# A second set of seven block products in the feed-forward pairs of a two-block transformer kernel

## The reference, cut to what matters

```python
hf = rms_norm(x, g_ffn)
x = x + (jax.nn.silu(hf @ w_gate) * (hf @ w_up)) @ w_down
```

## Time and profile before

| | |
|---|---|
| median of 3 runs | 2374.46 us (2371.44 to 2374.56) |
| profiled execution, own time | 2376.75 us |
| its span, first to last instruction | 2375.0 us |
| PE, DVE, ACT, POOL busy | 2365.2, 1861.1, 1193.0, 188.4 us |
| granted TensorE clock | 1.0 |
| unit copies to w_hi / subtractions to w_lo | 795 / 796 |

### The profile page before, as it was taken

One profiled execution on the slowest core, in us unless ns is written; L12 is line 12 of the kernel. 1 busy time (PEld: TensorE's weight loads), 2 busy tenths in 40 slices (PEclk: granted clock), 3 DMA queues, 4 the chain that ended last, 5 costly groups with the idle time before them and its releaser, 6 DMA issues.

```text
span 2375.0 us, 30803 instructions
## 1 busy us (share of the span) xinstructions
PE 2365.2 (100%) x10764; PEld 1968.8 (83%) x10764; DVE 1861.1 (78%) x2518; ACT 1193.0 (50%) x1615; POOL 188.4 (8%) x146
## 2 busy tenths in 40 slices
PE   9999999999999999999999999999999999999999
PEld 7988888788888888888888888888888888888887
DVE  7788887877677866878897977987867786687885
ACT  6554555544444544545564445454444454454563
POOL 1000000100211212100000000010121111210000
PEclk9999999999999999999999999999999999999999
DMA  8655555565655555656556564566565565564655
GB/s 304 238 173 186 168 169 174 189 212 188 202 195 197 195 187 195 206 167 199 184 194 195 181 221 160 194 223 195 187 204 195 195 195 189 193 211 161 208 192 168
DMA packets 126495, 462.24 MB, mean 195 GB/s; under 512 B 13712, under 2 KB 14352, under 8 KB 125728
## 3 DMA queue, kind: packets, MB, share of 16 engines
q1 hardware_dynamic: 116736, 421.32, 53.7%
q0 software_dynamic: 9344, 38.85, 4.8%
q10 hardware_dynamic: 288, 0.33, 0.0%
HBM read 458.35 MB, written 2.10 MB: 194 GB/s over the span
## 4 chain that ended last, share of the span: by engine, by line
PE 97%; DVE 2%; ACT 0%; DMA 0%; issue 0%; SPq 0%; ACTq 0%; DVEq 0%
PE acc L602 66%; PE pt L602 11%; PE po L602 11%; PE acc L750 2%; PE pt L750 2%; PE po L750 1%; PE acc L951 1%; PE acc L607 1%; PE po L934 1%; PE acc L865 1%; PE po L926 1%; DVE w_lo L1614 0%; PE pt L905 0%; PE acc L880 0%; DVE tmp_b L1749 0%; DVE tmp_c L1749 0%
## 5 line engine op out<-in xcount | busy, mean ns | idle before, releaser
L1614 DVE TENSOR_TENSOR w_lo<-raw,w_hi 128x1024 fp32r<-128x1024 f32 x796 | 992.2, 1258 | 424.8 <-ACT w_hi L1106 417.9
L1106 ACT ACTIVATE w_hi<-raw 128x1024 fp32r<-128x1024 f32 x795 | 836.6, 1058 | 936.1 <-PE acc L602 605.6
L602 PE MATMUL acc<-w_hi,norm_hi 128*128 128x512 f32 (+1 forms) x1524 | 593.6, 390 | 0.3 <-ACT w_hi L1106 0.2
L602 PE MATMUL acc<-w_hi,norm_lo 128*128 128x512 f32 (+1 forms) x1524 | 590.2, 388 | 0.0
L602 PE MATMUL acc<-w_lo,norm_hi 128*128 128x512 f32 (+1 forms) x1524 | 404.9, 388 | 0.9 <-DVE w_lo L1614 0.9
L602 PEld LDWEIGHTS acc<-w_hi,norm_hi 128*128 128x128 f32 x1524 | 286.1, 188 | 59.2 <-ACT w_hi L1106 1.0
L602 PEld LDWEIGHTS acc<-w_lo,norm_hi 128*128 128x128 f32 x1524 | 284.8, 188 | 60.3 <-DVE w_lo L1614 2.2
L602 PEld LDWEIGHTS acc<-w_hi,norm_lo 128*128 128x128 f32 x1524 | 286.2, 188 | 57.6
L602 PE MATMUL acc<-w_hi,mix_hi 128*128 128x512 f32 x848 | 330.9, 390 | 1.3 <-DVE mix_lo L2100 1.1
L602 PE MATMUL acc<-w_hi,mix_lo 128*128 128x512 f32 x848 | 330.0, 389 | 0.0
L602 PE MATMUL acc<-w_lo,mix_hi 128*128 128x512 f32 x848 | 226.8, 389 | 0.0
(11 more groups left out here) (312 smaller groups left out, 2513.7 us busy)
## 6 DMA issues: line engine op xcount, KB each, us to landing
raw<-stream SPq DMA_DIRECT2D x795, 512.0 KB, 3.5
heads<-seven_in POOLq DMA_DIRECT2D x24, 1024.0 KB, 6.7
heads<-x_in POOLq DMA_DIRECT2D x4, 512.0 KB, 8.3
x<-x_tok POOLq DMA_DIRECT2D x4, 512.0 KB, 7.3
x<-mem_tok POOLq DMA_DIRECT2D x2, 1024.0 KB, 6.6
x<-x_tok POOLq DMA_DIRECT2D x1, 2048.0 KB, 8.7
heads<-rows_in POOLq DMA_DIRECT2D x2, 1024.0 KB, 9.4
heads<-decay_in POOLq DMA_DIRECT2D x4, 512.0 KB, 5.3
```

The costliest lines, as they stand in the source:

```text
L602: last = pe.matmul(out_[:, c * NB:c * NB + width], a[:, k * T + c * P:k * T + (c + 1) * P], w[:, s, kk * width:(kk + 1) * width], start=cl ...
L1106: act.activation(w_hi[:, (units.fixed - 1) % RING, :], src, ACT.Copy).then_inc(w_hi_ready, 1)
L1614: dve.tensor_tensor(w_lo[:, s, :], src, w_hi[:, s, :].bitcast(F32), ALU.subtract)\
```

## The change

In the 24 pairs, the second unit of each block is also done by seven products. `STEPS = 2` sets now lie side by side in `heads`. Per pair PE has: `open_seven` with 8 products (24 matmuls, two steps of 12, the second behind a wait of its own), `close_seven` with 2 products (one for each set, 6 matmuls) and, in the same function, two units from the stream, each holding two tiles and used by 2 products (6 matmuls). Then 12 ordinary units of 12 matmuls. The pair still has 14 units in the stream. POOL loads 8 tiles (2 MB, in three DMAs) once `open_seven` of the pair before is done (`products_done`); the fourth tile of both sets lies alternately in `heads` and `tab`. DVE makes the four tile differences of the first set, between two of its splits, and POOL those of the second. ACT makes high parts in three instructions (4, 4 and 2 tiles), DVE low parts in three. The activation sums are twice as wide. Two loads (`tables`, rows of `g_final`, later `p_in` and the bias rows) and `gained_tables` move behind the last pair of their feed-forward.

Of the hunks below, those from `seven_hi` to the first `steps` lines are ACT's; those from `seven_sums` on are DVE's.

```diff
-SEVEN_CUTS = ((0, 5), (5, 7))
+SEVEN_CUTS = ((0, 4), (4, 6))
...
             def load_seven(j):
-                pool.dma_start(heads[:, L_TILE * T:L_TILE * T + 8 * NB].rearrange("p (a n) -> p a n", a=2)[:, :, 0:2 * NB],
-                               seven_in[j].rearrange("p (a n) -> p a n", a=2)).then_inc(seven_landed, 16)
+                for step in range(STEPS):
+                    pool.dma_start(raw7(step, W11, 3), seven_in[j][:, step * 4 * NB:(step * 4 + 3) * NB])\
+                        .then_inc(seven_landed[step], 16)
+                pool.dma_start(last_raw(j), seven_in[j].rearrange("p (s n) -> p s n", s=STEPS)[:, :, 3 * NB:])\
+                    .then_inc(last_landed, 16)
...
             for j in range(N_SEVEN):
                 if j:
-                    pool.wait_ge(seven_used, j)
+                    pool.wait_ge(products_done, j)
...
             def open_seven(j, act, ready):
 
                 c11, c12, c21, c22 = quarters_of(j)
                 pe.wait_ge(block_taken, first_of(j) - 2)
-                pe.wait_ge(seven_ready, 2 * j + 1)
                 pe.wait_ge(act_ready, sums_needed(j))
-                products(j, ((c11, "a11", W11), (c22, "s1", T1), (c12, "s2", T2), (c21, "s3", T3)), act, ready, True)\
-                    .then_inc(products_done, 1)
+                pe.wait_ge(*ready)
+                for step in range(STEPS):
+                    pe.wait_ge(seven_ready, 3 * j + step + 1)
+                    w = [(hi7(step, i), lo7(step, i)) for i in range(4)]
+                    last = products(j, step, ((c11, "a11", w[W11]), (c22, "s1", w[T1]), (c12, "s2", w[T2]),
+                                              (c21, "s3", w[T3])), act, step == 0)
+                last.then_inc(products_done, 1)
...
             def close_seven(j, act, ready):
 
                 c11, c12, c21, c22 = quarters_of(j)
-                pe.wait_ge(seven_ready, 2 * j + 2)
+                pe.wait_ge(seven_ready, 3 * j + 3)
                 pe.wait_ge(combined, j + 1)
                 pe.wait_ge(third_copied, j + 1)
-                products(j, ((c11, "a21", W21), (c12, "s4", W22), (c21, "a22", T4)), act, ready, False)\
-                    .then_inc(seven_used, 1)
+                pe.wait_ge(*ready)
+                for step in range(STEPS):
+                    last = products(j, step, ((c21, "a22", (last_hi()[:, step], last_lo(j)[:, step])),), act, False)
+                last.then_inc(seven_used, 1)
+                for step in range(STEPS):
+                    units.add()
+                    slot = (units.fixed - 1) % RING
+                    pe.wait_ge(w_hi_ready, units.value())
+                    pe.wait_ge(raw_read, units.value())
+                    one, two = ((w_hi[:, slot, at], w_lo[:, slot, at]) for at in (slice(0, NB), slice(NB, 2 * NB)))
+                    products(j, step, ((c11, "a12", one), (c12, "s4", two)), act, False).then_inc(w_used, 1)
...
-                            one_block(NU - 1, norm, k0=UK, token_major=True, opened=True)
-                            one_block(NU - 1, norm, k0=UK, token_major=True, opened=True,
-                                      mid=opening(pair, 3))
+                            one_block(NU - STEPS, norm, k0=STEPS * UK, token_major=True, opened=True)
+                            one_block(NU - STEPS, norm, k0=STEPS * UK, token_major=True, opened=True,
+                                      mid=opening(pair, 2))
...
             def seven_hi(j, part):
...
-                if part == 0:
-                    act.wait_ge(seven_summed, j + 1)
-                act.activation(hi7(first, n), raw7(first, n), ACT.Copy).then_inc(seven_hi_ready, 1)
+                if part < STEPS:
+                    act.wait_ge(seven_summed[part], j + 1)
+                    act.activation(hi7(part, W11, 4), raw7(part, W11, 4), ACT.Copy).then_inc(seven_hi_ready, 1)
+                else:
+                    if j:
+                        act.wait_ge(seven_used, j)
+                    act.activation(last_hi(), last_raw(j), ACT.Copy).then_inc(seven_hi_ready, 1)
...
-                            sums = {5: [lambda: sums_hi(which, False)], NU - 1: [gated]}
-                            steps(2 * NU, both(early, sums, preparing(after, 6), joining(after, 13)))
+                            sums = {7: [lambda: sums_hi(False), gated]}
+                            steps(2 * NU, both(early, preparing(after, 5, 6, 8), sums, joining(after, 13)))
...
-                            steps(2 * NU - 2, both(early, preparing(after_, 5), {NU - 2: [gated]}, sums, ready_))
+                            steps(2 * NU - 2, both(early, preparing(after_, 4, 6, 7), {NU - 1: [gated]}, sums, ready_))
...
+            def seven_sums(j):
+
+                dve.wait_ge(seven_landed[0], 16 * (j + 1))
+                dve.tensor_tensor(raw7(0, T3), raw7(0, T2), raw7(0, T1), ALU.subtract)
+                link(dve.tensor_tensor(raw7(0, T1), raw7(0, T1), raw7(0, W11), ALU.subtract))
+                link(dve.tensor_tensor(raw7(0, T2), raw7(0, T2), raw7(0, T1), ALU.subtract))
+                dve.wait_ge(last_landed, 16 * (j + 1))
+                dve.tensor_tensor(last_raw(j)[:, 0], last_raw(j)[:, 0], raw7(0, T2), ALU.subtract)\
+                    .then_inc(seven_summed[0], 1)
...
-                def preparing(j, at, behind=3):
+                def preparing(j, *at):
 
                     if j is None:
                         return {}
-                    return {at + behind: [lambda: seven_lo(j, 0)],
-                            at + behind + 1: [lambda: seven_lo(j, 1)]}
+                    return {at[0] - 2: [lambda: seven_sums(j)], **{k: [lambda i=i: seven_lo(j, i)] for i, k in enumerate(at)}}
...
-                            sums = {3: [lambda: sums_raw(which, False, which * N_SEVEN)],
-                                    6: [lambda: sums_lo(which, False)], NU - 1: [gated], 2 * NU - 1: [take_up]}
-                            steps(2 * NU, both(early, preparing(after, 5), joining(after, 13), sums))
+                            sums = {7: [lambda: sums_raw(False, which * N_SEVEN), gated],
+                                    9: [lambda: sums_lo(False)], 2 * NU - 1: [take_up]}
+                            steps(2 * NU, both(early, preparing(after, 6, 8, 10), joining(after, 13), sums))
...
-                            steps(2 * NU - 2, both(early, preparing(after, 3), sums, ready_, ends_))
+                            steps(2 * NU - 2, both(early, preparing(after, 5, 7, 8), sums, ready_, ends_))
```

More of the change, by code:

```diff
@@ L299, in two_blocks @@
         act_done = sem("act_done")
-        seven_landed = sem("seven_landed")
-        seven_summed = sem("seven_summed")
+        seven_landed = [sem(f"seven_landed{i}") for i in range(STEPS)]
+        last_landed = sem("last_landed")
+        seven_summed = [sem(f"seven_summed{i}") for i in range(STEPS)]
         seven_hi_ready = sem("seven_hi_ready")
@@ L735, in two_in_parts, with products @@
                         one_block(n_units, act, token_major=True, need=need, part=range(at, end), back=back * (i > 0))
[L737 to L741, removed]
+            def products(j, step, terms, act, clear):
+                sums = sums_at(hidden_sums(j))
+                for bank, of, (w_hi_, w_lo_) in terms:
                     if of[0] == "a":
-                        k, t = int(of[1]) - 1, int(of[2]) - 1
+                        k, t = step * UK + int(of[2]) - 1, int(of[1]) - 1
                         at = slice(k * T + t * P, k * T + (t + 1) * P)
@@ L746, in products @@
                     else:
[L747 to L750, removed]
+                        at = step * NB + (int(of[1]) - 1) * P
+                        a_hi, a_lo = (heads_r[:, (sums + i) * T + at:(sums + i) * T + at + P] for i in (0, 4))
+                    for i, (w, a) in enumerate(((w_hi_, a_hi), (w_hi_, a_lo), (w_lo_, a_hi))):
+                        last = pe.matmul(bank, a, w, start=clear and i == 0, stop=i == 2, skip_group_check=True)
                 return last
@@ L819, in mlp @@
                         else:
-                            after = lambda ki: down(ki + 1)
+                            after = lambda ki: down(ki + STEPS)
                             close_seven(j, mix, hidden_ready[g])
-                            for i, (at, end) in enumerate(SEVEN_CUTS if p == 0 else ((0, nd - 1),)):
+                            for i, (at, end) in enumerate(SEVEN_CUTS if p == 0 else ((0, nd - STEPS),)):
                                 for back in (1, 0):
-                                    one_block(nd - 1, mix, k0=UK, token_major=True, need=after, part=range(at, end),
-                                              back=back * (i > 0), opened=True,
-                                              mid=opening(pair, 4 if p == 0 else 2) if not i + back else None)
+                                    then = None
+                                    if (i, back) == ((1, 1) if p == 0 else (0, 0)):
```

(14 more changed lines are left out.)

148 lines of the change are left out of this document (87 added, 61 removed).

## The result

| | median us | runs | profiled execution, span |
|---|---|---|---|
| before | 2374.41 | 4 | 2376.75, 2375.0 |
| after | 2395.64 (2392.72 to 2397.22) | 4 | 2395.52, 2393.7 |

The change makes the kernel slower: 1.0091 of the time before, interval 1.0078 to 1.0103, or +21.2 us. 2396.8 was forecast.

The account below looks back on a forecast made before the run. PE bounds the kernel: number of matmuls times their distance, plus its waits. -16.3 - 1.8 + 27.6 + 1.6 + 11.2 = +22.3 us makes the median 2396.8; range 2372 to 2411, the forecast's own 2387 to 2411.

Parts of the forecast that it names:

- waits in g0 down 1 gone: Two waits at the openings in g0 down 1, for late tiles, vanish because POOL loads earlier: -1.8 us.
- 12 transposing pairs: Six pairs per feed-forward that also transpose wait 2.3 us each, 27.6; g1 up 3 starts late, 1.6 more.
- g0 up 1, twice: Once per feed-forward, PE waits 2.6 at unit 12 and 3.0 at the opening; 5.6 taken, twice: 11.2 us.
- first pair: First 2 MB load of each feed-forward, against gained_tables leaving it: taken as nothing, between -1 and +3.
- The order as the cause: DVE's work fits the fullest pair as a sum; program order behind the transposes makes PE wait.
- Both waits per pair: Transposing pairs: 0.4 to 1.2 us for w_hi of unit 9, another 1.27 for w_lo of unit 10.
- The forecast's formula: Unit 9's w_hi comes at X + 6.9, wanted at 20.40; unit 10's w_lo adds 1.27: 1.7 to 3.0 us.
- X: End of the transposes in a transposing pair, counted from the close's first matmul: between 13.9 and 15.2 us.
- Rival C: POOL's doubled load displaces the stream, X moves by 1 to 2 in 12 pairs: 2415 us; chance 0.05.
- It fits as a sum; the order decides: DVE's load in the fullest pair reaches 41.9 of 42.2 us, so instruction order decides.
- Rival A: The sums are never waited for, only the matmuls count: 2374.5 - 18.1 = 2356.4 us; chance 0.11.
- Rule of the port: VectorE two-input and GpSimd SBUF instructions exclude each other; one meeting costs 0.87 us, a second up to 0.5 more.

Follow-up runs that it names:

- order_only: Changed kernel; in the up pairs ACT's first-set high parts moved behind split 5, DVE's low parts behind splits 6, 7, 8: 2371.76 us, 0.9992 of the kernel before.
- sums_early: Changed kernel, g0 up 1 alone reordered: activation sums ahead of the transposes, tile parts mostly one split later; 2382.61 us, 1.0037 of the kernel before.
- with both: Changed kernel with the reorderings of order_only and sums_early, and DVE's tile sums behind split 4: 2360.61 us, 0.9945 of the kernel before.
- dve_both: Changed kernel with DVE making the tile sums of both sets, one behind the other, and POOL none: 2403.55 us, 1.0126 of the kernel before.
- load_late: Changed kernel with POOL issuing its loads behind the close (seven_used), not behind products_done: 2448.63 us, 1.0325 of the kernel before.
- pool_both: Changed kernel with POOL making the tile sums of both sets and DVE none, positions unchanged: 2376.77 us, 1.0011 of the kernel before.

## Why the prediction was right

The terms, against what the pairs measured (a pair's length is the distance between the first matmuls of successive closes):

| term | predicted | measured |
|---|---|---|
| 72 matmuls | -16.3 | -16.3 (light pairs 42.84 to 42.16) |
| waits in g0 down 1 gone | -1.8 | -1.5 (32.84 and 32.53 to 31.26 and 31.24) |
| 12 transposing pairs | 27.6 + 1.6 | 26.7 (1.6 to 3.6 each) |
| g0 up 1, twice | 11.2 | 13.2 (5.8 and 7.4) |
| first pair | 0 | -3.1 in the profiles |
| sum | +22.3 | +19.0, spans +18.7 |

- The order as the cause was right: the same work in another order gives back 23.9 of the 26.7 us (order_only), 13.0 of the 13.2 (sums_early) and 35.0 with both.
- Both waits per pair were right in place and size: 0.76 and 1.28 us in g1 up 2, against 0.4 to 1.2 and 1.27. The forecast's formula, X + 6.9 - 20.4 + 1.27 (X is the end of the transposes, counted from the close), gives the extra length of every transposing pair over 42.16 to within 0.2 us, each time 0.1 to 0.2 too high: 2.0 for X = 14.20 in g1 up 2 (1.8 measured), 2.8 for 15.02 in g2 up 2 (2.6), 3.8 for 16.01 in g1 up 3 (3.6).
- X itself spread more than foreseen. It lies at 14.0 to 15.2 in ten pairs (13.9 to 15.2 forecast) and at 15.6 and 16.0 in g1 up 3. POOL began its sums 1.6 us ahead of the close to 5.5 behind it, in seven of the twelve pairs at 4 to 5.5 (4 to 6 forecast). So seven pairs have 1.6 to 1.9 us and five 2.5 to 3.6, where the forecast had 2.3 for all, and 3.1 in g1 up 3.
- Not foreseen: in those five pairs a wait of 0.6 to 1.2 us at the `w_lo` of unit 8. It is due 19.5 behind the close, and split 4, behind the sums, ends at X + 5.05, so the wait comes when X passes 14.4. It is within what the formula gives for that X, since it moves the later deadlines too. g1 up 3 has another of 0.2 and 0.6 at unit 7.
- Rival C was too small for the time, but its sign is there: copies of ACT wait for the stream's DMA, in g1 up 3 for 2.48 and 2.09 us. Beside POOL's 2 MB two stream loads took 8.5 and 8.4 us there, against 3.5 at the median. In dve_both, without sums on POOL, X is still 15.1 and 14.6 in g1 up 3 and 13.87 in the other ten, so the late stream is worth about 1 us in these two pairs; VectorE, late with the units before, has a share in it that no run separates. The copy in the first feed-forward:

```profile
769.53 1.06 ACT L1139 ACTIVATE w_hi<-raw 128x1024 fp32r<-128x1024 f32 x1 [2.48 <-DMA raw<-stream]
```

- g0 up 1 was sized at 2.6 and 3.0. In the second feed-forward it is 2.8 and 3.2. In the first the second wait is just 1.7, since unit 12 itself took 1.4 longer, on the slow clock. The slow matmuls, 1.4 and 1.6 us in the two feed-forwards, are the part of this term that the sum left out. That the sum came so close is in part luck: the transposing pairs were 2.5 us too high and g0 up 1 2.0 too low.
- "It fits as a sum; the order decides" holds. The sum itself, 41.9 us in the fullest pair, was too high: 39.0 and, in the second feed-forward, 40.0 us were measured there, in pairs of 43.95 and 44.89.
- Taking the change in the median from the profile's own waits was off by the 3 us of the first pair: the profiled execution of before was slower than most. It did no harm, since the forecast put that term at nothing and counted from the median: without the row of the first pair the measured terms give +22.1, and the medians moved by 21.2.
- Rival A had the right size for another kernel: with both orders mended the time is 2360.6, against its 2356.4.
- Rule of the port (the Trainium skill, SBUF — State Buffer, "Who interferes with whom": a VectorE instruction with two SBUF inputs and a GpSimd one that reads SBUF exclude each other): the trace agrees, but one meeting a pair at 0.87 us was not what came. Five transposing pairs have one slowed subtraction of DVE ahead of X, at 1.48 to 1.55 us instead of 1.23, and seven have two, at 1.34 to 2.31. In load_late seven of the eight sums meet.

## What to carry to other kernels

When the bound engine's work shrinks, every deadline behind it moves forward: set the helpers' order against the new timetable, unit by unit, before adding work to them. A helper engine can be far from full and still set the time, by one instruction that waits in front of an urgent one; moving it behind the urgent one gave back 23.9 us here without taking any work away. Look also at which helpers run side by side: an early load may matter because it keeps two engines apart. And price a wait of the bound engine with what follows it: in load_late slow matmuls behind the waits are more than a third of the loss.

## What the runs showed of the hardware

TensorE fell to its lower level behind waits in the middle of a busy stretch. The window over the slow matmuls of the changed kernel has 0.54 in the clock's column (the number behind POOL's), so 1.2 GHz for most of it:

```profile
507.00:510.60 3.60, 3.41 (x9) 2.69 (x10) 3.43 (x3) 3.60 (x5) 0.00 (x0) 0.54 0.23 71
```

Distances between matmuls were 0.427 us there for 7 matmuls. In dve_both a wait of 3.4 us was followed by 13 such matmuls (granted clock 0.50 in a window over them), one of 4.6 by 7. In all these kernels, from 12 us on, no wait of 1.5 to 2.18 us had any behind it and each of the 13 from 3.0 us up had 4 to 13. In between it went both ways: one of 2.20 in pool_both was followed by 7 and one of 2.75 in the changed kernel by 7, but one of 2.81 in its second g0 up 1 and one of 2.92 in dve_both by none. Behind that 2.81 a wait of 3.2 came 5.7 us later and had 7.

Two-input subtractions of VectorE and of GpSimd, all within SBUF, take turns by whole instructions. Where both engines ran 512-wide ones (load_late), they took 1.67 to 1.78 us instead of 0.69 on VectorE and 1.62 instead of 1.29 on GpSimd. Beside VectorE's wider ones GpSimd's took longer, 2.15 us beside a 1024-wide and 3.22 where a 2048-wide and a 1024-wide followed each other (pool_both). VectorE's stream transposes kept 0.44.

GpSimd's 2 MB in three DMAs landed 8.4 to 14.4 us after the first issue in the changed kernel, where 1 MB in one had taken 6.2 to 9.1.
